# Forgetting attention's heads turned inside the quarters of the weight units, with their copies shared by two engines; two more pieces of work moved

## The reference, cut to what matters

```
def fox_mixer(h, w_in, b_f, q_gain, k_gain, w_out):
    proj = h @ w_in
    q, k, v, gate, f_logit = (the columns of proj)
    q = rmsnorm(heads(q), q_gain)          # over the 64 numbers of a head
    k = rmsnorm(heads(k), k_gain)
    c = jnp.cumsum(log_sigmoid(f_logit + b_f), axis=1)
    s = einsum('bhqd,bhkd->bhqk', q, k) * HEAD_DIM ** -0.5
    s = s + c[query] - c[key]
    p = softmax(where(query >= key, s, -inf))
    o = einsum('bhqk,bhkd->bhqd', p, v) * sigmoid(gate)
    return o @ w_out
```

## Time and profile before

| | us |
|---|---|
| median of 3 runs | 1047.97 |
| the runs | 1047.97, 1043.12, 1048.05 |
| the profiled execution, its own time | 1044.04 |
| its span, first to last instruction | 1042.3 |
| TensorE busy | 997.6 |
| VectorE busy | 638.2 |
| ScalarE busy | 480.8 |
| GpSimd busy | 347.8 |

### The profile page before, as it was taken

How to read it: one execution, slowest core, us unless ns; L and a number is a source line. 1 busy time by engine, 2 the same in 40 slices (tenths; PEclk the granted TensorE clock), 3 DMA queues, 4 the chain that set the end, 5 groups by cost and what they waited for, 6 DMA issues and landing times.

```text
span 1042.3 us, 16880 instructions
## 1 busy us (share of the span) xinstructions
PE 997.6 (96%) x6874; PEld 882.7 (85%) x6874; DVE 638.2 (61%) x656; ACT 480.8 (46%) x628; POOL 347.8 (33%) x325
## 2 busy tenths in 40 slices
PE   8998899999999898989999999999979999999997
PEld 6975679999988776878789999987957989999985
DVE  4999766666664453554666775535766575555534
ACT  6771455444443455455454434434434554343432
POOL 5792037898899222220029940000100010000000
PEclk9996899999999999999999999999999999999999
DMA  9741035677666845454355555555980546565540
GB/s 337 249 159 41 1 122 184 216 225 219 225 230 222 255 127 176 135 159 141 112 176 168 175 187 175 188 201 185 403 320 3 177 148 195 169 198 167 197 162 40
DMA packets 130081, 186.84 MB, mean 179 GB/s; under 512 B 4720, under 2 KB 103536, under 8 KB 129392
## 3 DMA queue, kind: packets, MB, share of 16 engines
q1 hardware_dynamic: 106032, 158.61, 46.6%
q10 hardware_dynamic: 24000, 27.54, 7.8%
HBM read 174.60 MB, written 15.73 MB: 183 GB/s over the span
## 4 chain that ended last, share of the span: by engine, by line
PE 77%; DVE 13%; ACT 4%; issue 2%; DMA 2%; POOL 0%; ACTq 0%; DVEq 0%; POOLq 0%
PE ps L394 13%; PE ps L396 13%; PE ps L395 13%; PE ps L443 7%; PE ps L445 7%; PE ps L447 7%; DVE cacc L1808 4%; PE ps L415 4%; PE ps L417 3%; PE ps L416 3%; DVE wlo L354 3%; ACT whi L348 2%; DMA wraw<-in_s_w_glu 2%; PE ps L821 1%; PE ps L840 1%
## 5 line engine op out<-in xcount | busy, mean ns | idle before, releaser
L354 DVE TENSOR_TENSOR wlo<-wraw,whi 128x2048 fp32r<-128x2048 f32 x143 | 345.5, 2416 | 237.5 <-ACT whi L348 237.5
L348 ACT ACTIVATE whi<-wraw 128x2048 fp32r<-128x2048 f32 x143 | 273.8, 1914 | 379.3 <-PE ps L396 217.9
L394 PE MATMUL ps<-actH,whi 128*128 128x256 f32 x1232 | 351.6, 285 | 2.7 <-DVE wlo L354 1.5
L396 PE MATMUL ps<-actH,wlo 128*128 128x256 f32 x1232 | 348.6, 283 | 0.0
L395 PE MATMUL ps<-actL,whi 128*128 128x256 f32 x1232 | 348.6, 283 | 0.0
L394 PEld LDWEIGHTS ps<-actH,whi 128*128 128x128 f32 x1232 | 236.3, 192 | 6.2 <-issue 4.0
L395 PEld LDWEIGHTS ps<-actL,whi 128*128 128x128 f32 x1232 | 236.4, 192 | 0.1
L396 PEld LDWEIGHTS ps<-actH,wlo 128*128 128x128 f32 x1232 | 236.4, 192 | 0.0
L594 POOL TENSOR_SCALAR rs<-ss 128x1 f32<-128x1 f32 (+2 forms) x16 | 4.7, 291 | 583.3 <-ACT nat L580 473.9
L443 PE MATMUL ps<-whi,gH 128*128 128x512 f32 x264 | 81.9, 392 | 0.0
L445 PE MATMUL ps<-wlo,gH 128*128 128x512 f32 x264 | 81.4, 389 | 0.0
(11 more groups left out here) (341 smaller groups left out, 1391.1 us busy)
## 6 DMA issues: line engine op xcount, KB each, us to landing
wraw<-in_ffn_w_gate SPq DMA_DIRECT2D x22, 1024.0 KB, 5.4
wraw<-in_ffn_w_up SPq DMA_DIRECT2D x22, 1024.0 KB, 5.4
wraw<-in_ffn_w_down SPq DMA_DIRECT2D x22, 1024.0 KB, 4.9
wraw<-in_fox_w_in SPq DMA_DIRECT2D x16, 1024.0 KB, 5.4
wraw<-in_w_gate SPq DMA_DIRECT2D x11, 1024.0 KB, 5.4
wraw<-in_w_up SPq DMA_DIRECT2D x11, 1024.0 KB, 5.5
wraw<-in_w_down SPq DMA_DIRECT2D x11, 1024.0 KB, 4.9
wraw<-in_w_in SPq DMA_DIRECT2D x9, 1024.0 KB, 11.3
```

Source lines behind the costliest of these rows:

```text
L348: act.activation(self.whi[:, n0 % RING, :], self.wraw[:, n0 % RAW, :], ACT.Copy).then_inc(self.hi_done, 1)
L354: dve.tensor_tensor(self.wlo[:, n0 % RING, :], self.wraw[:, n0 % RAW, :], self.whi[:, n0 % RING, :].bitcast(F32), ALU.subtract).then_inc(s ...
L394: pe.matmul(out, wh, self.actH[:, k, :], start=(i == 0), stop=False)
L396: last = pe.matmul(out, wl, self.actH[:, k, :], start=False, stop=(i == KT - 1))
```

## The change

1. The fills of the fox heads are no longer in one block. The four fills of keys 0 to 7 stand after the second quarter of unit 5 and go to banks 2 to 5; the four of queries 0 to 7 stand behind unit 5, in banks 0 to 3. Of keys 8 to 15, one fill stands before quarter 22 of `others_a`, the others around the last steps of the first half of attention; quarter 23 moves behind the turn of head 7. The queries 8 to 15 stand behind that.
2. The copies of these fills are shared: ScalarE makes 4 + 2 of the first eight and 1 + 4 of the second, VectorE 2 and 3. A copy now multiplies by the gain, one number for each of the 66 rows, so GpSimd's multiplication by the gain goes; the factor 1/8 of the queries goes into VectorE's normalisation, which becomes a three-operand instruction for queries.
3. On ScalarE a small exponential stands ahead of the key copies of the first half; the split of unit 7 (ScalarE and VectorE) and that of unit 13 (VectorE) stand later.
4. In the first attention ScalarE copies the turned probabilities, not VectorE. The eight power table copies stand with heads 3 to 6, two each.
5. GpSimd makes the S5 phases right behind the last head norm of the fox stage, ahead of the norms "pm0" and "f2". Their scratch space moves to where `D0` lies.

The diff, cut to its core:

```diff
+    def act_probs_turned(self, act, st, g, pt, tb):
+        act.wait_ge(*self.past(st + "_turned", g + 1))
+        if g >= 2:
+            act.wait_ge(*self.past(st + "_out", g - 1))
+        act.activation(pt[:, g % 2, :], self.ps[:, tb[g % 2], 0:384], ACT.Copy).then_inc(self.sem(st + "_pt"), 1)
...
+    def pe_head_fill(self, pe, name, src, h, bank):
+        w = src.shape[-1]
+        for i in range(2):
+            for r in range(RT):
+                c = (2 * i + r) * P
+                last = pe.transpose(self.ps[0:w, bank, c:c + P], src[:, r, h + i, :], self.ident[:])
+        last.then_inc(self.sem(name + "_turned"), 1)
...
+    def act_head_copy(self, act, name, f, bank):
+        ready, out, src, gain = self.head_copy(name, f, bank)
+        act.wait_ge(*ready)
+        act.activation(out, src, ACT.Copy, scale=gain).then_inc(self.sem(name + "_out_a"), 1)
+
+    def dve_head_copy(self, dve, name, f, bank):
+        ready, out, src, gain = self.head_copy(name, f, bank)
+        dve.wait_ge(*ready)
+        dve.tensor_scalar(out, src, gain, None, ALU.mult).then_inc(self.sem(name + "_out_d"), 1)
...
@@ GpSimd @@
+            for i in range(4):
+                if i > 0:
+                    pool.wait_ge(*m.past("head_normed", 2 * i))
                 m.pool_rstd(pool, f"blk{i}", HD, f"blk{i}_head_sums", 16)
-                for r in range(RT):
-                    pool.wait_ge(*m.past("head_normed", 2 * i + r + 1))
-                    v = t[:, r, 8 * (i // 2):8 * (i // 2) + 8, 0:HD]
-                    pool.tensor_tensor(v, v, m.qkg[:, g:g + 1, :].to_broadcast([P, 8, HD]), ALU.mult)\
-                        .then_inc(sem("gained"), 1)
+            pool_s5_phases(m, c, pool)
             m.pool_rstd(pool, "pm0", D, "pm0_squares")
             m.pool_rstd(pool, "f2", D, "f2_squares", out=m.rx)
-            pool_s5_phases(m, c, pool)
...
@@ TensorE @@
+            m.mm_half_k(pe, n + 4, (6, 7), 0)
+            for k in range(4):
+                m.mm_quarter(pe, n + 5, (6, 7), 1, k)
+                if k == 1:
+                    pe.wait_ge(*m.past("c_cols", 4))
+                    pe.wait_ge(*m.past("bias_ones", 4))
+                    pe.wait_ge(*m.past("fox_out", 4))
+                    pe.wait_ge(*m.past("head_normed", 2))
+                    for f in range(4):
+                        m.pe_head_fill(pe, "keys", m.ka, 2 * f, 2 + f)
+            pe.wait_ge(*m.past("head_normed", 4))
+            for f in range(4):
+                if f >= 2:
+                    pe.wait_ge(*m.past("keys_out_a", f - 1))
+                m.pe_head_fill(pe, "queries", m.qa, 2 * f, f)
...
-            m.pe_heads(pe, "a2", m.ka, (0, 8), "gained", 2, (2, 3), 0)
-            m.pe_heads(pe, "a2", m.qa, (0, 8), "gained", 4, (2, 3), 4)
-            pe.wait_ge(*m.past("a2_heads_out", 8))
-            pe.wait_ge(*m.past("fox_out", 6))
...
+                if i == 22:
+                    pe.wait_ge(*m.past("head_normed", 6))
+                    m.pe_head_fill(pe, "keys", m.ka, 8, 0)
...
+            def tail_a(i):
+                if i == 0:
+                    m.pe_head_fill(pe, "keys", m.ka, 10, 1)
+                    m.mm_quarter(pe, n + 11, (6, 7), 1, 3)
+                if i == 1:
+                    pe.wait_ge(*m.past("a2_pt", 7))
+                    m.pe_head_fill(pe, "keys", m.ka, 12, 2)
+                if i == 2:
+                    pe.wait_ge(*m.past("a2_pt", 8))
+                    m.pe_head_fill(pe, "keys", m.ka, 14, 3)
...
-            m.pe_heads(pe, "a2", m.ka, (8, 16), "gained", 6, (2, 3), 8)
-            m.pe_heads(pe, "a2", m.qa, (8, 16), "gained", 8, (2, 3), 12)
-            pe.wait_ge(*m.past("a2_heads_out", 16))
+            pe.wait_ge(*m.past("head_normed", 8))
+            for f in range(4):
+                pe.wait_ge(*(m.past("keys_out_d", f + 1) if f < 3 else m.past("keys_out_a", 5)))
+                m.pe_head_fill(pe, "queries", m.qa, 8 + 2 * f, f)
...
@@ ScalarE, first attention @@
             for h in range(H1):
+                if h > 0:
+                    m.act_probs_turned(act, "a1", h - 1, m.pt1, (6, 7))
                 m.act_attention(act, "a1", h, m.p1, rsum, nmax, (4, 5))
+                if h == H1 - 1:
+                    m.act_probs_turned(act, "a1", h, m.pt1, (6, 7))
-                if h > 5:
+                if 3 <= h < 7:
...
@@ ScalarE, fox stage @@
+                if i == 2:
+                    act.activation(m.nmax[:, 0, 0:1], m.halfpi[:], ACT.Exp)
+                    for f in range(4):
+                        m.act_head_copy(act, "keys", f, 2 + f)
                 block_out(i, ((0, 1), (4, 5), (6, 7))[i])
+                if i == 2:
+                    for f in (2, 3):
+                        m.act_head_copy(act, "queries", f, f)
                 m.split_high(act, n + 2 * i + 3)
...
+                    if h == 7:
+                        m.act_head_copy(act, "keys", 7, 3)
+                        for f in range(4):
+                            m.act_head_copy(act, "queries", 4 + f, f)
                     m.split_high(act, n + j + 2)
...
@@ VectorE @@
-            m.dve_attention(dve, "a1", (0, H1), m.pt1, nmax, (4, 5), (6, 7), conv_part)
+            m.dve_attention(dve, "a1", (0, H1), None, nmax, (4, 5), (6, 7), conv_part)
...
+                if i == 2:
+                    for f in range(2):
+                        m.dve_head_copy(dve, "queries", f, f)
+                else:
+                    m.split_low(dve, n + 2 * i + 3)
...
+                if h == 0:
+                    m.split_low(dve, n + 7)
+                if h == 7:
+                    m.dve_head_copy(dve, "keys", 4, 0)
+                if h == 8 and not second:
+                    for f in (1, 2):
+                        m.dve_head_copy(dve, "keys", 4 + f, f)
+                    return
```

More of the change, by code:

```diff
@@ L845, in pe_attention @@
             if h < h1:
+                if ready:
+                    ready(h)
                 scores(h)
@@ L878, in dve_attention @@
                        .then_inc(self.sem(st + "_max"), 1)
-            if h > h0:
+            if h > h0 and pt is not None:
                 g = h - 1
@@ L903, in pe_heads, with head_copy @@
                 between(f)
+    def pe_head_fill(self, pe, name, src, h, bank):
[5 more added lines that the diff above has]
+        last.then_inc(self.sem(name + "_turned"), 1)
+    def head_copy(self, name, f, bank):
+        dst, gain = {"keys": (self.kt2, FOXK), "queries": (self.qt2, FOXQ)}[name]
+        w = HD + 2
+        return (self.past(name + "_turned", f + 1), dst[:, 2 * f:2 * f + 2, :],
+                self.ps[0:w, bank, :].rearrange("p (h t) -> p h t", h=2), self.vec[0:w, gain:gain + 1])
+    def act_head_copy(self, act, name, f, bank):
[6 more added lines that the diff above has]
+        dve.tensor_scalar(out, src, gain, None, ALU.mult).then_inc(self.sem(name + "_out_d"), 1)
     def act_heads(self, act, st, dst, heads, banks, first_fill):
@@ L1341, in _ @@
                     last.then_inc(sem("f_turned"), 1)
-            for i, banks in ((1, (4, 5)), (2, (6, 7))):
-                for h in range(2):
-                    m.mm_half_k(pe, n + 2 * i + h, banks, h)
-                if i == 1:
-                    pe.wait_ge(*m.past("logf", 1))
-                    lf = m.fl[:, 1]
-                    pe.matmul(ps[:, 2, 0:H2], m.tri[:], lf[:, 0, :], start=True, stop=True)
-                    pe.matmul(ps[:, 2, H2:2 * H2], m.ones[:], lf[:, 0, :], start=True, stop=False)
-                    pe.matmul(ps[:, 2, H2:2 * H2], m.tri[:], lf[:, 1, :], start=False, stop=True)\
-                      .then_inc(sem("csum"), 1)
@@ L1369, in _ @@
-            pe.wait_ge(*m.past("a2_pt", 8))
-            m.pe_heads(pe, "a2", m.ka, (8, 16), "gained", 6, (2, 3), 8)
-            m.pe_heads(pe, "a2", m.qa, (8, 16), "gained", 8, (2, 3), 12)
-            pe.wait_ge(*m.past("a2_heads_out", 16))
-            pe.wait_ge(*m.past("fox_out", 12))
+            for h in range(2):
+                m.mm_half_k(pe, n + 2 + h, (4, 5), h)
+            pe.wait_ge(*m.past("logf", 1))
+            lf = m.fl[:, 1]
+            pe.matmul(ps[:, 2, 0:H2], m.tri[:], lf[:, 0, :], start=True, stop=True)
@@ new lines, in _ @@
+            pe.matmul(ps[:, 2, H2:2 * H2], m.ones[:], lf[:, 0, :], start=True, stop=False)
+            pe.matmul(ps[:, 2, H2:2 * H2], m.tri[:], lf[:, 1, :], start=False, stop=True).then_inc(sem("csum"), 1)
+            m.mm_half_k(pe, n + 4, (6, 7), 0)
[8 more added lines that the diff above has]
+                        m.pe_head_fill(pe, "keys", m.ka, 2 * f, 2 + f)
@@ L2000, in others @@
                         dve.tensor_tensor(t, t, m.ga[:, r, 0:512], ALU.mult).then_inc(sem("fo_gated"), 1)
+                if h == 0:
+                    m.split_low(dve, n + 7)
[4 more added lines that the diff above has]
+                        m.dve_head_copy(dve, "keys", 4 + f, f)
+                    return
                 if h in (7, 15, 16):
                     return
```

(2 more changed lines are left out.)

74 lines of the change are left out of this document (43 added, 31 removed).

## The result

| | before | after |
|---|---|---|
| median of five runs of each, taken together, us | 1047.66 | 1036.09 |
| the profiled execution, its own time | 1044.04 | 1034.07 |
| its span | 1042.3 | 1032.4 |

The ratio is 0.9916, with a 95% interval of 0.9891 to 0.994: faster by 8.8 us (6 to 11). The medians in the table differ by 11.6, a ratio of 0.989 just outside that interval: they rest on five runs each. In 41 further executions of the kernel before, beside the experiments, the median was 1045.1, against which 1036.09 is 0.991. Predicted were 1036.5, and 9.6 us between the two profiled executions; these differ by 9.97.

The account below looks back on a forecast made before the run. PE was taken as the bound: busy 96% of the span, 77% of the chain. The terms 4.7 + 2.1 + 4.0 - 2.5 + 1.3 = 9.6 us took 1044.04 to 1034.4; two added for the median gave 1036.5, range 1030 to 1044.

Parts of the forecast that it names:

- Part A: First eight head fills of the fox stage: PE no longer waits for copies, saving 4.7 us (bounds 3.5 and 5.0).
- Part B: Second eight head fills, ahead of the second half of fox attention: saving 2.1 us (bounds 1.0 and 2.7).
- Part C: GpSimd's gain multiplications taken off and the factor 1/8 moved: worth nothing.
- Part D: First attention: 2.4 us from copies leaving DVE, 1.6 from a kept clock; saving 4.0 (bounds 1.5 and 6).
- 1.2 us for the new last wait: First attention: PE's wait for the last probabilities shrinks to 1.2 us, so the clock was taken as kept.
- Rival 2: First attention: clock unchanged or PE sets the pace, so it gives 1.5 to 2.4 us; time 1038.5, chance 0.22.
- Part E: Moved S5 phases beside the end of fox attention slow DVE's instructions: 2.5 us lost (bounds 0 and 8).
- about 1.5 us: Slack in PE's order for the low parts and first-half gate, each late by up to 1.9 us beside the phases.
- Rival 1: Phases fall fully on the end of fox attention, delaying both gate multiplications: 8 us lost, time 1042, chance 0.20.
- Part F: Second feed-forward network without the phases: two PE gaps behind low parts go, saving 1.3 us (bounds 1.0 and 1.5).
- Rival 3: Fox head copies stay on the path, the two fill blocks together giving 2 us, not 6.8; time 1041, chance 0.10.
- rival 4: Phases on POOL make pm0's norm late: slower, 1050 us if they last 85 or more; chance 0.03.

Follow-up runs that it names:

- x1_phases_back: The kernel after with GpSimd's S5 phases put back behind the norms pm0 and f2, as before; ratio to before 0.9876.
- x6_last_warm: x1_phases_back plus ten extra bf16 matmuls in PE's wait ahead of the turn of head 7 in the first attention; ratio to before 0.9832, median 1028.67 us.
- x10_fills_block: x1_phases_back with the first four key fills moved behind unit 5, so eight fills stand in one block; ratio to before 0.9885.
- x7_chop_ffn: x1_phases_back with the long GpSimd instructions of the phases cut to at most 256 columns (496 for the copy); ratio to before 0.9859.
- x8_chop_fox: The kernel after, phases in the fox stage, their long GpSimd instructions cut to at most 256 columns (496 for the copy); ratio to before 0.9867.
- x11_best: x1_phases_back with the edits of x7_chop_ffn and x6_last_warm together; ratio to before 0.9856.
- x12_best_warm: x11_best plus ten more bf16 matmuls in PE's wait ahead of unit 0 of the fox stage; ratio to before 0.9861, median 1030.69 us.

## Why the prediction was right, and where not

The time was right to 0.4 us and the sum of the parts to 0.4, but with luck, by errors that cancel: the gains of A, B, D and F were put too small by 2.5 (12.1 for 14.6) and the loss of E by 2.7. A, B and F came out above their own bounds (5.0, 2.7 and 1.5).

- **Part A**, 4.7 predicted, 5.6 measured. The mechanism holds: no gap, all copies hidden, unit 7's split (402.96) not missed. The mis-sized terms are 0.52 for a fill, read from two fills that were followed by a wait, where four in a row take 0.435 each, and 0.3 for changes between kinds of matmul. 9.18 less 3.48 is 5.7. That some 0.9 of the 9.18 was the lower clock behind the wait of 2.76 was not seen, but the sum did not need it. What I also did not see is that the key fills need not have moved into unit 5.
- **Part B**, 2.1 predicted, 3.4 measured, outside its bound of 2.7. The fills at 0.435 explain 0.8 of the 1.3 (6.42 less 3.48, and nothing for changes, is 2.9). The last 0.4 lies around the key fills: the twelve value matmuls of heads 6 and 7 took 1.54 us in one row before (460.15 to 461.69) and take 0.62 and 0.62 with a fill between them, and two fills beside quarters take 0.35 each, not 0.435. ACT's copy behind unit 11's values was no problem.
- **Part C**, 0 predicted. No run tests it alone.
- **Part D**, 4.0 predicted, 3.8 measured in after and 2.7 in x1_phases_back, about 3.3 over ten profiles. The step on DVE is right, and better than charged: six copies are 2.8 us of the last maximum, without the 0.4. The step on the clock was right for after only, and its reason was wrong. "1.2 us for the new last wait" holds in no profile: where DVE gives the whole 2.8, PE waits 2.6 and the clock falls (3.73 for the channel sum); where PE is held up by an earlier stretch at the lower level, it waits 0.90, the clock is kept, and half of DVE's gain is not seen. No profile has both, until the wait is filled (x6_last_warm), and x10_fills_block has part of the first and nothing of the second (36.86 and 9.90). Rival 2, that the clock stays as it is, came true in those executions, though its 1.5 to 2.4 is a little low for them.
- **Part E**, 2.5 lost predicted, 5.2 measured. This is the step that failed. The length (54 predicted, 54.5 measured), the slowness of long instructions and pm0's 23.6 us of slack were right. The slack of "about 1.5 us" was right as well: in x1_phases_back the maximum of head 15 starts at 490.00 and its turn at 493.30, 3.3 later, where after needs 1.6 (493.41 to 495.02), so 1.7 is spare. Wrong was to hold each lateness against it alone. The low part and the gate stand on one list and add up: the maximum of head 14 comes 2.2 later than in x1_phases_back, the gate puts 3.1 on top, and 5.3 less 1.7 is the 3.6 by which the last turn is late. The last gate lost 1.6 and not 3.4. Together that is the 5.2, with nothing left for the clock. Rival 1 had the right kind of loss, both instructions of a gate pair and late low parts, but saw the pair at the end of attention; its 8 was as far off as the 2.5.
- **Part F**, 1.3 predicted, 1.8 measured. The two gaps of PE were the right ones, but I took their length from the brackets, which count from modelled ends. From start to start they are 0.79 and 1.10 (602.16 to 602.95, 608.69 to 609.79) where neighbours stand 0.12 apart, and the first matmul behind each takes 0.22: together 1.85. x7_chop_ffn reaches the same 192.50 with the phases in place.
- **Rival 3** (head copies on the path) and **rival 4** (pm0 late) did not come about. Rival 4 comes within 1.6 us once the phases are cut small in the fox stage.

The remaining 0.5 of the sum (1.1 gained in the S5 mixer, 0.6 lost at the start) is no part of the change: the mixer takes 114.0 to 115.9 over all these profiles with its code unchanged.

## What to carry to other kernels

A long GpSimd instruction beside VectorE ones with two SBUF inputs is priced by its length and by what stands behind the held-up one on VectorE's list, not by GpSimd's busy time: cut it to pieces of the size of VectorE's work before looking for another place for it (the cut gave back 4.7 us in the place that the change chose, 1.8 in the old one). When several instructions on one list are late, add their delays before you hold them against a slack. When a change makes an engine give its result earlier, ask what TensorE's wait there grows to; a gain of 2.8 us was paid back in clock until ten matmuls filled the wait. And where an engine waits for a copy, look first at what stands ahead of the copy on its engine and at how many banks take turns: sharing the copies was worth 0.9 and moving the first fills into the unit nothing.

## What the runs showed of the hardware

- Nearly the same wait of PE, 2.8 to 3.2 us ahead of unit 0, was followed by 0, 3.4 or 6.1 us at the lower level in different profiles (x7_chop_ffn 0 behind 3.05, after 3.4 behind 2.91, x8_chop_fox 6.1 behind 2.95), and one of 5.19 by 3.4 (x6_last_warm). The length of a wait alone did not decide it. Filled down to 0.72 it was followed by none.
- Transposes of 66 columns in an unbroken row take 0.109 us each from start to start at the upper level; the busy time of a pair of fills gave 0.13.
- On 64 partitions, GpSimd's multiplication by a constant takes 5.70 us for 2048 columns in one instruction and 10.67 for the same in eight (1.33 each); a two-input instruction of 960 columns takes 1.93, one of 256 0.82.
- One store of 256 KB landed 5.2 us after its issue in two profiles (x6_last_warm, x11_best) and 2.8 to 3.0 in three others (x1_phases_back, x7_chop_ffn, x12_best_warm), with the same code around it.
